# Expert layers: half of the first up product placed ahead of the last two picks, and the loop rotated behind it

## The chip, the cores and the metric

The kernel runs on one core of one Trainium2 chip. The metric is the device time of one execution in microseconds, given as the median of the timed runs; less is better. The engines are TensorE (PE, with its weight loads as PEld), VectorE (DVE), ScalarE (ACT), GpSimd (POOL) and SyncE (SP, which issues the loads).

## The reference

The program is two blocks of two layers each over 512 tokens of width 1024. The change touches only the mixture of experts that closes each layer of the second block. Cut to that part:

```python
def hier_moe(h, w_grp, b_grp, w_rt, b_rt, w_up, w_down):
    ...
    x_pad = jnp.zeros((rows, dm), h.dtype).at[dest].set(xt[tok])
    ...
    def expert_block(args):
        xb, e = args
        gate_up = xb @ w_up[e]
        a, u = jnp.split(gate_up, 2, axis=-1)
        return (jax.nn.silu(a) * u) @ w_down[e]
    ...
    y = y_pad.reshape(rows, dm)[dest] * w_sorted[:, None].astype(h.dtype)
    return jnp.zeros_like(xt).at[tok].add(y).reshape(bsz, length, dm)
```

Every token goes to 2 of 32 experts. An expert multiplies its tokens by an up matrix (1024 x 1024: 512 columns for the gate, 512 for the values), forms silu(gate) times value, and multiplies by a down matrix (512 x 1024). The first such layer works on 528 tokens (16 meta tokens and 512 others), the second on 512.

## The kernel before

`stage_experts` computes one such layer, and it stands twice in the program: layer 0 with five token tiles (`T` is 5), layer 1 with four. All 32 experts are computed one after the other for up to 64 tokens each (tokens beyond 64 go through a later part that runs only where there are some). Two experts are a pair, since 128 columns of a one-hot matrix pick the tokens of two experts at once.

The steps of a pair `p`, and who does them:

- VectorE compares slot numbers with a row of numbers (`match`, L3881) and adds the two maps (`join`, L3887, signal `onehot`): a one-hot matrix `row`.
- TensorE multiplies the tokens by `row` (`pick`, L3892): eight chunks of 128 channels, for each chunk `T` matmuls. Chunks 0 to 3 go to one PSUM bank (signal `turned[0]`), chunks 4 to 7 to another (`turned[1]`).
- VectorE copies a bank to SBUF with the norm's gain (`place(0)`, `place(1)`, L3897, signals `placed[0]`, `placed[1]`). The picked tokens then stand transposed in `xT`.
- For each of the two experts, TensorE does the up product in two halves of four chunks (`tensor_up`, L3903). Half 0 reads what `place(0)` wrote, half 1 what `place(1)` wrote. Behind half 0 the signal `half_up` rises, behind half 1 `up_ready`.
- ScalarE takes the Silu (L4127, signal `silu`), VectorE multiplies (L4210, signal `hid`), TensorE transposes (`tensor_hidden`, L3908), ScalarE copies (L4131, signal `h_placed`), TensorE does the down product (`tensor_down`, L3915, signal `dn_ready`), VectorE copies the result out of PSUM (L4223), and ScalarE issues two stores of it.

The order on each engine is written by hand. On TensorE the picks of the next pair are spread through the current one: two chunks behind an up product, two behind the transposes. Before the loop TensorE runs all eight picks of pair 0 in one go. The loop (`pe.Fori(0, 5)`, six experts in its body) then begins with half 0 of expert 0. `last_pair` is written out behind the loop.

On VectorE, ahead of its loop, stand `place(0)`, `place(1)`, the `join` for the next pair, and then `route.overflow` (18 small steps, L3803 to L3832), which works out which experts have more than 64 tokens. VectorE takes its instructions in order, so its loop, with the multiplication L4210 of expert 0, begins behind all of that.

SyncE issues the loads of the weights, also in order. Up weights have three buffers, each loaded in two halves of 2048 KB (L3460); down weights have two buffers, 2048 KB each (L3463). The loads of the first experts are issued during the routing. In the loop:

```python
def load_up(e, b):
    sp.wait_ge(half_up.sem, e + (half_up.base - 2))
    weights.load_up(sp, e, b, 0).then_inc(up_in[b][0].sem, 16)
    sp.wait_ge(up_ready.sem, e + (up_ready.base - 2))
    weights.load_up(sp, e, b, 1).then_inc(up_in[b][1].sem, 16)
```

So half 0 of expert 3 is loaded when expert 0 has done its half 0, half 1 when expert 0 has done its up product, and then the down weights of expert 2 when `dn_ready` of expert 0 has risen.

Of the kernel before, what the change touches and what calls it, by code (L numbers as in the profile page):

```python
# [37 lines left out]
NEXP, GROUPS, EPG, DFF = 32, 4, 8, 512  # L38
# [3804 lines left out]
def stage_experts(g, layer, tiles, keep, gw, dest, slot, over, weights, gains, route, finish):  # L3843
# [11 lines left out]
    up_in, dn_in, y_free = weights.up_in, weights.down_in, (y_free0, y_free1)  # L3855
    turned, placed = (turned0, turned1), (placed0, placed1)
# [42 lines left out]
    def tensor_up(n, b, half):  # L3899
        wv = up[b].rearrange("p k (s q c) -> p k q s c", s=2, q=2)  # L3900
        for k in range(4 * half, 4 * half + 4):
            for q in range(2):
                last = nc.tensor.matmul(g.psum[64 * q:64 * q + 64, 2 + n, :].rearrange("p (s c) -> p s c", s=2), xT[:, k // 4, k % 4, ROWS * n:ROWS * n + ROWS], wv[:, k, q, :, :], start=k == 0, stop=k == KD - 1)  # L3903
        return last
# [69 lines left out]
    with nc.Block() as block:  # L3974
# [39 lines left out]
        def _(pe):  # L4014
            route.tensor(pe)

            def expert(p, n, turn_up, turn_down, b, more):

                if n == 0:
                    pe.wait_ge(placed[0].sem, p + (placed[0].base + 1))  # L4020
                pe.wait_ge(up_in[b][0].sem, 16 * turn_up + (up_in[b][0].base + 16))
                tensor_up(n, b, 0).then_inc(half_up.sem, 1)
                if n == 0:
                    pe.wait_ge(placed[1].sem, p + (placed[1].base + 1))
                pe.wait_ge(up_in[b][1].sem, 16 * turn_up + (up_in[b][1].base + 16))
                tensor_up(n, b, 1).then_inc(up_ready.sem, 1)
                if more:
                    if n == 0:
                        pe.wait_ge(onehot.sem, p + (onehot.base + 2))
                    pick((4 * n, 4 * n + 1))  # L4030
                pe.wait_ge(hid.sem, 2 * p + (hid.base + n + 1))
                tensor_hidden().then_inc(h_turned.sem, 1)
                if more:
                    pick((4 * n + 2, 4 * n + 3)).then_inc(turned[n].sem, 1)
                pe.wait_ge(h_placed.sem, 2 * p + (h_placed.base + n + 1))
                pe.wait_ge(dn_in[n].sem, 16 * turn_down + (dn_in[n].base + 16))
                tensor_down(n, n).then_inc(dn_ready.sem, 1)

            def last_pair():

                p = PAIRS - 1
                first, second = NEXP - 2, NEXP - 1
                for half in range(2):
                    pe.wait_ge(placed[half].sem, p + (placed[half].base + 1))
                    pe.wait_ge(up_in[first % 3][half].sem, 16 * (first // 3) + (up_in[first % 3][half].base + 16))
                    last = tensor_up(0, first % 3, half)
                last.then_inc(up_ready.sem, 1)
                pe.wait_ge(up_in[second % 3][0].sem, 16 * (second // 3) + (up_in[second % 3][0].base + 16))
                tensor_up(1, second % 3, 0)
                pe.wait_ge(hid.sem, hid.base + first + 1)  # L4050
                tensor_hidden().then_inc(h_turned.sem, 1)
                pe.wait_ge(*gated.at(2))
                for n in range(2):
                    for i in range(4):
                        last = turn_gates(i, n, (n, i * P))
                if T > 4:
                    for n in range(2):
                        last = turn_gates(4, n, (5, n * P))
                last.then_inc(*g_turned.up())
                pe.wait_ge(up_in[second % 3][1].sem, 16 * (second // 3) + (up_in[second % 3][1].base + 16))  # L4060
                tensor_up(1, second % 3, 1).then_inc(up_ready.sem, 1)
                pe.wait_ge(h_placed.sem, h_placed.base + first + 1)
                pe.wait_ge(dn_in[0].sem, 16 * p + (dn_in[0].base + 16))
                tensor_down(0, 0).then_inc(dn_ready.sem, 1)
                pe.wait_ge(hid.sem, hid.base + second + 1)
                tensor_hidden().then_inc(h_turned.sem, 1)
                pe.wait_ge(h_placed.sem, h_placed.base + second + 1)
                pe.wait_ge(dn_in[1].sem, 16 * p + (dn_in[1].base + 16))
                tensor_down(1, 1).then_inc(dn_ready.sem, 1)
# [12 lines left out]
                    to_tokens(i, picked[1], y_last[1], False, True).then_inc(*combined.up())  # L4082

            pe.wait_ge(onehot.sem, onehot.base + 1)
            for n in range(2):
                pick(range(4 * n, 4 * n + 4)).then_inc(turned[n].sem, 1)
            with pe.Fori(0, 5) as i:
                for j in range(6):
                    expert(3 * i + j // 2, j % 2, 2 * i + j // 3, 3 * i + j // 2, j % 3, True)
            count = blocks_over(pe)  # L4090
            last_pair()

# [204 lines left out]
            sig.count = 16 * len(range(b, NEXP, 3))  # L4297
    for sig in dn_in:
        sig.count = 16 * PAIRS
    half_up.count = NEXP - 2  # L4300
    for sig in (up_ready, hid, silu, h_turned, h_placed, dn_ready, y_placed):
        sig.count = NEXP
    for sig in y_free:
# [872 lines left out]
```

## Time and profile before

| | |
|---|---|
| median of 3 runs | 2619.38 us |
| lowest and highest run | 2616.13 and 2620.86 us |
| span of the profiled execution | 2617.4 us (the profile gives no other time for this execution) |
| TensorE busy | 2477.6 us, 95% of the span |
| TensorE weight loads busy | 1381.7 us, 53% |
| VectorE, ScalarE, GpSimd busy | 1091.8, 627.1, 580.7 us |
| DMA | 531.89 MB, 203 GB/s in the mean |
| mean granted TensorE clock | 0.987 of full speed |

The busy times are sums over the whole program; the two expert layers lie near 1221 to 1724 us and 2126 to 2608 us of the span. A busy TensorE is not one at its peak, since matmuls are pipelined and their ends are modelled. In the timeline, rows of equal instructions are merged: the number behind the x is how many, and the length runs from the first one's start to the last one's end. One matmul of the program is two rows in the trace, as the picks show: 40 in the program's order, 80 in the timeline.

### The profile page before, as it was taken

The page shows a single profiled execution, that of the slowest core. Times are in us where ns is not written, and L with a number is a line of the kernel's source. Part 1 is how long each engine was busy: PE and PEld are TensorE (multiplying, and loading weights), DVE is VectorE, ACT ScalarE, POOL GpSimd, SP SyncE. Part 2 cuts the span into 40 slices and gives each one's busy share as a digit, 9 for nine tenths or more (in the row PEclk, how much of TensorE's full clock was granted, in tenths as well). Part 3 has the DMA queues.
Part 4 walks back from the last instruction along what each step waited for, and adds up shares of the span by engine and source line. Part 5 has one row for each costly group of instructions (what it writes and reads, how often), then busy time and mean ns, then how long its engine had stood idle before and what let it go on. Part 6 is the DMA issues. An engine that isn't in the chain of part 4 may idle for free. (4 is left out here: it accounts for less than half of the span.)

```text
span 2617.4 us, 38917 instructions
## 1 busy us (share of the span) xinstructions
PE 2477.6 (95%) x15572; PEld 1381.7 (53%) x15572; DVE 1091.8 (42%) x2083; ACT 627.1 (24%) x1451; POOL 580.7 (22%) x688
## 2 busy tenths in 40 slices
PE   7997899999989999999999999989999899999998
PEld 4554445756644444546555555558555454545443
DVE  4636554554255554755111211264666541111113
ACT  2217113433311222812000001032455121000010
POOL 1734343462124231430000000020345200000001
PEclk9999999999999999999999999999999999999999
DMA  5121013110120411154999999851001369999998
GB/s 190 65 96 49 33 37 129 53 36 3 35 81 10 155 65 66 50 213 177 403 426 427 428 426 426 359 196 65 34 34 66 131 247 425 426 426 428 426 427 364
DMA packets 116730, 531.89 MB, mean 203 GB/s; under 512 B 23601, under 2 KB 33713, under 8 KB 83825
## 3 DMA queue, kind: packets, MB, share of 16 engines
q1 hardware_dynamic: 104624, 505.74, 48.1%
q10 hardware_dynamic: 9600, 15.74, 1.6%
q0 software_dynamic: 2368, 8.52, 0.9%
q8 instruction: 94, 1.54, 0.2%
q14 instruction: 44, 0.35, 0.0%
HBM read 507.26 MB, written 22.58 MB: 202 GB/s over the span
## 5 line engine op out<-in xcount | busy, mean ns | idle before, releaser
L3903 PE MATMUL psum<-arena,hidden_T 128*64 128x512 f32 x1376 | 303.0, 592 | 0.0
L3892 PEld LDWEIGHTS psum<-hidden_T,arena 128*128 128x128 f32 x2304 | 266.6, 192 | 51.5 <-issue 51.5
L3892 PE MATMUL psum<-hidden_T,arena 128*128 128x128 f32 x2304 | 283.5, 278 | 1.2 <-DVE hidden_T L3887 1.2
L3915 PE MATMUL psum<-weight_ring,hidden_T 128*64 128x512 f32 x1024 | 233.7, 598 | 13.4 <-DMA weight_ring<-in_moe_w_down 10.1
L3903 PEld LDWEIGHTS psum<-arena,hidden_T 128*64 128x64 f32 x1376 | 100.6, 137 | 193.2 <-issue 193.1
L3897 DVE TENSOR_TENSOR hidden_T<-psum,norm_gains 128x512 f32<-128x512 f32 x64 | 44.3, 692 | 295.5 <-PE psum L3903 182.7
L4127 ACT ACTIVATE hidden_T<-psum 128x256 f32<-128x256 f32 x64 | 24.6, 385 | 530.5 <-PE psum L3903 530.5
L3903 PE MATMUL psum<-weight_ring,hidden_T 128*64 128x512 f32 x672 | 147.9, 592 | 0.0
L3915 PEld LDWEIGHTS psum<-weight_ring,hidden_T 128*64 128x64 f32 x1024 | 69.2, 136 | 131.6 <-issue 118.7
L4175 POOL DMA_INDIRECT arena<-expert_rows_out,arena x10 | 12.0, 1199 | 502.5 <-DMA expert_rows_out<-arena 499.7
L4573 PE MATMUL psum<-weight_ring,hidden_T 128*128 128x512 f32 x256 | 122.1, 606 | 0.3 <-DVE arena L4931 0.3
L4175 POOL DMA_INDIRECT weight_ring<-expert_rows_out,arena x8 | 8.1, 1012 | 483.6 <-DMA expert_rows_out<-arena 481.4
L337 POOL TENSOR_TENSOR arena<-arena,constants 128x1 f32<-128x1 f32 (+6 forms) x90 | 102.8, 1142 | 7.5
L4210 DVE TENSOR_TENSOR hidden_T<-hidden_T,psum 128x256 f32<-128x256 f32 x60 | 25.0, 416 | 186.5 <-ACT hidden_T L4127 186.5
L3903 PEld LDWEIGHTS psum<-weight_ring,hidden_T 128*64 128x64 f32 x672 | 49.0, 137 | 94.6 <-issue 94.5
L333 POOL TENSOR_SCALAR arena<-arena 128x1 f32<-128x1 f32 (+6 forms) x90 | 32.3, 359 | 286.7 <-DVE arena L3107 82.0
L4223 DVE COPY hidden_T<-psum 128x512 f32<-128x512 f32 x30 | 20.8, 692 | 179.8 <-PE psum L3915 179.8
L4127 ACT ACT_TABLE_LOAD x30 | 38.5, 1283 | 216.4 <-issue 216.3
L4769 POOL TENSOR_TENSOR weight_ring<-arena 128x256 f32<-128x256 f32 x56 | 41.7, 745 | 188.2 <-PE psum L4621 102.2
L445 PE MATMUL psum<-arena 128*128 128x512 f32 x160 | 70.6, 594 | 2.9 <-DVE hidden L550 2.9
L550 DVE TENSOR_TENSOR hidden<-hidden,psum 128x512 f32<-128x512 f32 x48 | 32.1, 684 | 95.1 <-PE psum L445 95.1
L347 PE MATMUL psum<-weight_ring,arena 128*128 128x512 f32 (+2 forms) x192 | 63.4, 454 | 6.0 <-PEq L1583 6.0
(646 smaller groups left out, 4391.6 us busy)
## 6 DMA issues: line engine op xcount, KB each, us to landing
arena<-in_moe_w_up SPq DMA_DIRECT2D x86, 2048.0 KB, 14.9
weight_ring<-in_moe_w_down SPq DMA_DIRECT2D x64, 2048.0 KB
weight_ring<-in_moe_w_up SPq DMA_DIRECT2D x42, 2048.0 KB, 14.8
weight_ring<-in_hg_w_in SPq DMA_DIRECT2D x8, 2048.0 KB, 11.6
weight_ring<-in_ev_w_in SPq DMA_DIRECT2D x8, 1536.0 KB, 8.9
weight_ring<-in_fox_w_in SPq DMA_DIRECT2D x6, 2048.0 KB, 11.8
weight_ring<-in_od_w_in SPq DMA_DIRECT2D x5, 2048.0 KB, 8.3
weight_ring<-in_ple_w_gate SPq DMA_DIRECT2D x4, 2048.0 KB, 8.9
```

The source lines that it names most:

```text
L333: g.nc.gpsimd.tensor_scalar(out, sums, scale, EPS, ALU.mult, ALU.add).then_inc(*chain.up())
L337: g.nc.gpsimd.tensor_tensor(out, out, power, ALU.pow).then_inc(*done.up())
L347: last = nc.tensor.matmul(out, l, r, start=i == 0, stop=i == len(left) - 1)
L445: last = nc.tensor.matmul(where[n](p), a[:, k, :], b[:, k, :], start=k == 0 and n in (1, 5, 6), stop=k == 3, skip_group_check=n in (2, 3, ...
L550: nc.vector.tensor_tensor(dst, dst, where[n](p), ALU.add).then_inc(*added.up())
L3892: last = nc.tensor.matmul(g.psum[:, c // 4, (c % 4) * P:(c % 4 + 1) * P], keep[:, i, c * P:(c + 1) * P], row[:, i, :], start=i == 0, stop= ...
L3897: return nc.vector.tensor_tensor(xT[:, a, :, :], g.psum[:, a, :].rearrange("p (k r) -> p k r", k=4), gain[:, 4 * a:4 * a + 4].unsqueeze(2) ...
L3903: last = nc.tensor.matmul(g.psum[64 * q:64 * q + 64, 2 + n, :].rearrange("p (s c) -> p s c", s=2), xT[:, k // 4, k % 4, ROWS * n:ROWS * n ...
L3915: last = nc.tensor.matmul(g.psum[64 * q:64 * q + 64, 6 + n, :], aT[:, k % 2, 64 * (k // 2):64 * (k // 2) + 64], down[b][:, k, 512 * q:512 ...
L4127: nc.scalar.activation(s, g.psum[:, 2 + n, 0:256], ACT.Silu).then_inc(silu.sem, 1)
L4573: last = mm(bank(u % 2), g.hT[:, k, a:a + n], w[:, k, :], **flags)
L4769: op(dv[:, :, 0, :], mid, bv[:, :, 0, :], ALU.subtract).then_inc(*subbed.up())
```

## The change

Ahead of the loop TensorE now runs picks 0 to 5, then half 0 of expert 0's up product, then picks 6 and 7. A function `first_half` holds half 0. In the loop body an expert that opens a pair begins with half 1, since its half 0 is done, and behind each expert that closes a pair half 0 of the next pair's first expert follows. `last_pair` begins with half 1 for the same reason, and half 0 of expert 30 now raises `half_up`, so its count is one higher. The parameter `more` was always true and is gone. No other engine's code is changed.

```diff
--- before.py
+++ after.py
@@ -4014,24 +4014,27 @@
         def _(pe):
             route.tensor(pe)
 
-            def expert(p, n, turn_up, turn_down, b, more):
+            def first_half(p, n, turn_up, b):
 
                 if n == 0:
                     pe.wait_ge(placed[0].sem, p + (placed[0].base + 1))
                 pe.wait_ge(up_in[b][0].sem, 16 * turn_up + (up_in[b][0].base + 16))
-                tensor_up(n, b, 0).then_inc(half_up.sem, 1)
+                return tensor_up(n, b, 0)
+
+            def expert(p, n, turn_up, turn_down, b):
+
                 if n == 0:
                     pe.wait_ge(placed[1].sem, p + (placed[1].base + 1))
+                else:
+                    first_half(p, n, turn_up, b).then_inc(half_up.sem, 1)
                 pe.wait_ge(up_in[b][1].sem, 16 * turn_up + (up_in[b][1].base + 16))
                 tensor_up(n, b, 1).then_inc(up_ready.sem, 1)
-                if more:
-                    if n == 0:
-                        pe.wait_ge(onehot.sem, p + (onehot.base + 2))
-                    pick((4 * n, 4 * n + 1))
+                if n == 0:
+                    pe.wait_ge(onehot.sem, p + (onehot.base + 2))
+                pick((4 * n, 4 * n + 1))
                 pe.wait_ge(hid.sem, 2 * p + (hid.base + n + 1))
                 tensor_hidden().then_inc(h_turned.sem, 1)
-                if more:
-                    pick((4 * n + 2, 4 * n + 3)).then_inc(turned[n].sem, 1)
+                pick((4 * n + 2, 4 * n + 3)).then_inc(turned[n].sem, 1)
                 pe.wait_ge(h_placed.sem, 2 * p + (h_placed.base + n + 1))
                 pe.wait_ge(dn_in[n].sem, 16 * turn_down + (dn_in[n].base + 16))
                 tensor_down(n, n).then_inc(dn_ready.sem, 1)
@@ -4040,11 +4043,9 @@
 
                 p = PAIRS - 1
                 first, second = NEXP - 2, NEXP - 1
-                for half in range(2):
-                    pe.wait_ge(placed[half].sem, p + (placed[half].base + 1))
-                    pe.wait_ge(up_in[first % 3][half].sem, 16 * (first // 3) + (up_in[first % 3][half].base + 16))
-                    last = tensor_up(0, first % 3, half)
-                last.then_inc(up_ready.sem, 1)
+                pe.wait_ge(placed[1].sem, p + (placed[1].base + 1))
+                pe.wait_ge(up_in[first % 3][1].sem, 16 * (first // 3) + (up_in[first % 3][1].base + 16))
+                tensor_up(0, first % 3, 1).then_inc(up_ready.sem, 1)
                 pe.wait_ge(up_in[second % 3][0].sem, 16 * (second // 3) + (up_in[second % 3][0].base + 16))
                 tensor_up(1, second % 3, 0)
                 pe.wait_ge(hid.sem, hid.base + first + 1)
@@ -4082,11 +4083,15 @@
                     to_tokens(i, picked[1], y_last[1], False, True).then_inc(*combined.up())
 
             pe.wait_ge(onehot.sem, onehot.base + 1)
-            for n in range(2):
-                pick(range(4 * n, 4 * n + 4)).then_inc(turned[n].sem, 1)
+            pick(range(4)).then_inc(turned[0].sem, 1)
+            pick((4, 5))
+            first_half(0, 0, 0, 0).then_inc(half_up.sem, 1)
+            pick((6, 7)).then_inc(turned[1].sem, 1)
             with pe.Fori(0, 5) as i:
                 for j in range(6):
-                    expert(3 * i + j // 2, j % 2, 2 * i + j // 3, 3 * i + j // 2, j % 3, True)
+                    expert(3 * i + j // 2, j % 2, 2 * i + j // 3, 3 * i + j // 2, j % 3)
+                    if j % 2:
+                        first_half(3 * i + j // 2 + 1, 0, 2 * i + (j + 1) // 3, (j + 1) % 3).then_inc(half_up.sem, 1)
             count = blocks_over(pe)
             last_pair()
 
@@ -4297,7 +4302,7 @@
             sig.count = 16 * len(range(b, NEXP, 3))
     for sig in dn_in:
         sig.count = 16 * PAIRS
-    half_up.count = NEXP - 2
+    half_up.count = NEXP - 1
     for sig in (up_ready, hid, silu, h_turned, h_placed, dn_ready, y_placed):
         sig.count = NEXP
     for sig in y_free:
```

On TensorE at the entry of layer 0's loop (names in brackets are the signals waited for: `rows_placed_0` and `rows_placed_1` are `placed`, `piece_loaded_0` and `piece_loaded_1` the two halves of the first up weights, `gated` is `hid`), before:

```order
L3892 MATMUL psum<-hidden_T,arena 128x128 [waits onehot_ready,rows_scaled]
L3892 MATMUL psum<-hidden_T,arena 128x128 x39
L4087 UNCONDITIONAL_BRANCH
L4087 ISA
L4021 ISA [waits rows_placed_0]
L3903 MATMUL psum<-weight_ring,hidden_T 64x512 [waits piece_loaded_0]
L3903 MATMUL psum<-weight_ring,hidden_T 64x512 x7
L3903 MATMUL psum<-weight_ring,hidden_T 64x512 [waits piece_loaded_1,rows_placed_1]
L3903 MATMUL psum<-weight_ring,hidden_T 64x512 x7
L4029 REGISTER_ALU
```

And now:

```order
L3892 MATMUL psum<-hidden_T,arena 128x128 [waits onehot_ready,rows_scaled]
L3892 MATMUL psum<-hidden_T,arena 128x128 x29
L3903 MATMUL psum<-weight_ring,hidden_T 64x512 [waits piece_loaded_0,rows_placed_0]
L3903 MATMUL psum<-weight_ring,hidden_T 64x512 x7
L3892 MATMUL psum<-hidden_T,arena 128x128 x10
L4090 UNCONDITIONAL_BRANCH
L4090 ISA
L4030 ISA [waits rows_placed_1]
L3903 MATMUL psum<-weight_ring,hidden_T 64x512 [waits piece_loaded_1]
L3903 MATMUL psum<-weight_ring,hidden_T 64x512 x7
```

Ten of the forty pick matmuls have moved behind the eight matmuls of half 0, and the wait for `rows_placed_1` has moved from a matmul in the middle of the up product to the sequencer, right behind the last picks and the branch into the loop.

On TensorE at the end of the same loop and the first rows of `last_pair` (L3959 reads the number of experts with more than 64 tokens), before:

```order
L3915 MATMUL psum<-weight_ring,hidden_T 64x512 [waits piece_loaded_7,hidden_placed]
L3915 MATMUL psum<-weight_ring,hidden_T 64x512 x7
L4087 REGISTER_ALU
L4087 COMPARE_AND_BRANCH
L3959 TENSOR_LOAD arena
L3959 ISA x2
L3903 MATMUL psum<-weight_ring,hidden_T 64x512 [waits piece_loaded_0,rows_placed_0]
L3903 MATMUL psum<-weight_ring,hidden_T 64x512 x7
```

And now:

```order
L3903 MATMUL psum<-weight_ring,hidden_T 64x512 [waits piece_loaded_0]
L3903 MATMUL psum<-weight_ring,hidden_T 64x512 x7
L4090 REGISTER_ALU
L4090 COMPARE_AND_BRANCH
L3959 TENSOR_LOAD arena
L3959 ISA x2
L3903 MATMUL psum<-weight_ring,hidden_T 64x512 [waits piece_loaded_1,rows_placed_1]
L3903 MATMUL psum<-weight_ring,hidden_T 64x512 x7
```

Half 0 of expert 30 (eight matmuls) has moved from behind the loop's closing branch and the read L3959 to ahead of them.

## Rows read from the trace of the kernel before

**Rows 1.** Timeline, ScalarE, both layers: start us, length us, engine, line, form, idle before.

```profile
1268.06 0.38 ACT L4127 ACTIVATE hidden_T<-psum 128x256 f32<-128x256 f32 x1 [3.24 <-PE psum L3903]
...
1298.72 0.39 ACT L4127 ACTIVATE hidden_T<-psum 128x256 f32<-128x256 f32 x1 [3.26 <-PE psum L3903]
...
2523.85 0.39 ACT L4127 ACTIVATE hidden_T<-psum 128x256 f32<-128x256 f32 x1 [3.25 <-PE psum L3903]
...
2554.57 0.38 ACT L4127 ACTIVATE hidden_T<-psum 128x256 f32<-128x256 f32 x1 [3.25 <-PE psum L3903]
```

**Rows 2.** Waits, TensorE, 1219 to 1700: who waited for whom: us, times, longest.

```profile
PE psum L3892 <- DVE hidden_T L3887: 0.9, 1, 0.9
```

**Rows 3.** Waits, TensorE, 2140 to 2617, columns as before.

```profile
PE psum L3915 <- DMA weight_ring<-in_moe_w_down: 10.1, 12, 1.0
```

**Rows 4.** Timeline, TensorE, the first wait for down weights in layer 1.

```profile
2405.65 3.65 PE L3915 MATMUL psum<-weight_ring,hidden_T 128*64 128x512 f32 x16 [0.57 <-DMA weight_ring<-in_moe_w_down]
```

**Rows 5.** Windows: stretch, length, busy us of PE, PEld, DVE, ACT, POOL; PEclk, DMA, GB/s.

```profile
2400.00:2545.00 145.00, 136.63 (x784) 72.20 (x782) 26.73 (x49) 12.83 (x24) 0.00 (x0) 1.00 1.01 427
```

**Rows 6.** Timeline, TensorE, entry of layer 0's expert loop.

```profile
1221.16 9.17 PE L3892 MATMUL psum<-hidden_T,arena 128*128 128x128 f32 x80 [0.91 <-DVE hidden_T L3887]
1230.26 7.09 PE L3903 MATMUL psum<-weight_ring,hidden_T 128*64 128x512 f32 x32
1237.28 2.50 PE L3892 MATMUL psum<-hidden_T,arena 128*128 128x128 f32 x20
1239.61 0.38 PE L3908 MATMUL psum<-constants,hidden_T 128*128 128x128 f32 x2
```

**Rows 7.** Timeline, TensorE, entry of layer 1's expert loop.

```profile
2126.82 7.38 PE L3892 MATMUL psum<-hidden_T,arena 128*128 128x128 f32 x64 [0.30 <-DVE hidden_T L3887]
2134.13 7.09 PE L3903 MATMUL psum<-arena,hidden_T 128*64 128x512 f32 x32
2141.15 2.05 PE L3892 MATMUL psum<-hidden_T,arena 128*128 128x128 f32 x16
2143.04 0.38 PE L3908 MATMUL psum<-constants,hidden_T 128*128 128x128 f32 x2
...
2148.62 7.04 PE L3903 MATMUL psum<-arena,hidden_T 128*64 128x512 f32 x32
```

**Rows 8.** Timeline, VectorE, entry of layer 0's expert loop.

```profile
1225.90 0.69 DVE L3897 TENSOR_TENSOR hidden_T<-psum,norm_gains 128x512 f32<-128x512 f32 x1 [2.37 <-PE psum L3892]
...
1230.37 0.69 DVE L3897 TENSOR_TENSOR hidden_T<-psum,norm_gains 128x512 f32<-128x512 f32 x1 [3.77 <-PE psum L3892]
...
1236.80 0.17 DVE L3832 CAST arena<-arena 128x17 int32<-128x17 f32 x1
1237.81 0.42 DVE L4210 TENSOR_TENSOR hidden_T<-hidden_T,psum 128x256 f32<-128x256 f32 x1 [0.84 <-ACT hidden_T L4127]
```

**Rows 9.** Timeline, VectorE, entry of layer 1's expert loop.

```profile
2134.24 0.69 DVE L3897 TENSOR_TENSOR hidden_T<-psum,norm_gains 128x512 f32<-128x512 f32 x1 [2.88 <-PE psum L3892]
...
2140.40 0.18 DVE L3832 CAST arena<-arena 128x17 int32<-128x17 f32 x1
2141.68 0.42 DVE L4210 TENSOR_TENSOR hidden_T<-hidden_T,psum 128x256 f32<-128x256 f32 x1 [1.11 <-ACT hidden_T L4127]
```

**Rows 10.** Timeline, SyncE's queue, the first down load of layer 1's loop.

```profile
2148.99 0.39 SPq L3463 DMA_DIRECT2D weight_ring<-in_moe_w_down  x1
```

**Rows 11.** Windows, right behind the first down load of layer 1's loop.

```profile
2150.00:2154.00 4.00, 4.00 (x22) 1.35 (x20) 0.00 (x0) 0.00 (x0) 0.00 (x0) 1.00 0.97 300
```

**Rows 12.** Timeline, TensorE, entry of the stage behind layer 0.

```profile
1737.37 1.97 PE L4621 MATMUL psum<-hidden_T,weight_ring 128*128 128x256 f32 x8 [1.64 <-PEq L3974]
```

**Rows 13.** Windows, within layer 1's routing.

```profile
2114.00:2118.00 4.00, 4.00 (x7) 1.61 (x6) 3.45 (x18) 1.07 (x2) 0.00 (x0) 0.57 0.99 420
```

**Rows 14.** Timeline, TensorE, 16 matmuls that hold the engine busy, layer 0 and layer 1.

```profile
1208.62 7.11 PE L359 MATMUL psum<-constants 128*128 128x512 f32 x16
...
2113.56 8.81 PE L359 MATMUL psum<-constants 128*128 128x512 f32 x16
```

## Prediction

> **What bounds the kernel now.** I looked first for the part of the span that the edit can touch: the two expert layers, some 480 us each. The Silu activations give the pace of an expert, since each expert has one. In layer 0 two experts take 1298.72 - 1268.06 = 30.66 us, and late in layer 1 they take 2554.57 - 2523.85 = 30.72 us [rows 1]. The paces are alike but the causes differ. In layer 0 TensorE waits once, 0.9 us, ahead of the first pick, and never again [rows 2], so the layer is as long as its matmuls. Layer 1 has four token tiles, not five, so its picks are shorter and its first expert needs only 2148.62 - 2134.13 = 14.49 us [rows 7]. It runs at its matmuls' pace until the first wait for down weights at 2405.65 [rows 4], and from there it has 12 such waits, 10.1 us in all [rows 3], at 427 GB/s [rows 5]. An expert moves three loads of 2048 KB and two stores of 128 KB, 6.55 MB, and 6.55 MB at 427 GB/s take 15.35 us, which is half of 30.70. So layer 0 is bound by TensorE, and layer 1 by a stream of loads that starts when its first buffers are given back.
>
> The place of the edit is the entry of each loop. There TensorE runs eight picks, then expert 0's up product in two halves, two picks, the hidden transposes (L3908), two picks, the down product. VectorE puts the picked blocks into place (`place(0)` and `place(1)`, L3897), then works through the overflow code (L3803 to L3832), and only then enters its own loop, whose first instruction is the gating product L4210 that the transposes wait for.
>
> **The change, part by part.** No matmul, load or copy is added or removed. What moves is the order at the entry, on TensorE alone; inside the loop the same order is written from another starting point.
>
> *Moved: first half ahead of the last two picks, layer 0.* The eight picks run from 1221.16 to 1230.26, 9.10 us, so two take 2.28 us. The up product runs from 1230.26 to 1237.28, so a half takes 3.51 us [rows 6]. In the new order the first half starts 2.28 us earlier, at 1227.98. Its operand is in place by then: `place(0)` ends at 1225.90 + 0.69 = 1226.59 [rows 8]. So this start costs no wait, and `half_up` rises 2.28 us earlier.
>
> *What it uncovers: `place(1)`.* Before, `place(1)` (0.69 us, from 1230.37, right behind the last pick) ran beside the first half, 3.51 us, and cost nothing [rows 6, 8]. Now the last picks stand behind the first half and end where the half ended before, near 1233.8, and the second half needs `place(1)` at once. Nothing is left on TensorE to cover it. I count 0.69 us for it; 0.11 us in front, since before it began that much behind the point at which TensorE could have gone on (1230.37 against 1230.26); and 0.1 us, an estimate from the same 0.11, for the hand-over back to TensorE: **0.9 us** of idle TensorE.
>
> *What is queued behind it on VectorE.* VectorE works in order, so the overflow code starts 3.51 us later too. Before, it ended at 1236.80 + 0.17 = 1236.97, 0.84 us ahead of L4210 [rows 8]; VectorE was waiting for the Silu. Now it ends at 1240.48. L4210 takes 0.42, so its product is there at 1240.90, and with 0.1 for the hand-over the transposes start at 1241.0, where they started at 1239.61 [rows 6]. That is a delay of **1.4 us**. The 0.9 us lie inside it: TensorE, 0.9 late, would have been at the transposes at 1240.5, and waits 0.5 more. The same sum for layer 1: the half is (2141.15 - 2134.13) / 2 = 3.51 us; the overflow code ends at 2140.40 + 0.18 + 3.51 = 2144.09; with 0.42 and 0.1 the transposes start at 2144.61 against 2143.04, **1.6 us** late [rows 7, 9].
>
> *The entry of VectorE's loop.* Branch and register work there was hidden in the idle time ahead of L4210, so the trace bounds it only: from nothing to 0.84 us (layer 0) and 1.10 us (layer 1, 2140.58 to 2141.68) [rows 8, 9]. I take 0.2 us in each layer, near the low end, for it is a few sequencer instructions. It adds 0.4 us in all.
>
> *Where the delay goes in layer 0.* TensorE sets the pace and has no idle time later to lose it in, so the whole 1.4 + 0.2 stays: +1.6 us.
>
> *Where it goes in layer 1, and what the early load is worth.* The load of expert 3's first half goes out when `half_up` rises, half an up product behind 2134.13, and would go out some 1.8 us earlier, two picks of layer 1 (2134.13 - 2126.82 = 7.31 us, a quarter of it) [rows 7]. The transfer can start then, since the queues are idle. But the queue that it stands in is in order: half 0 (behind `half_up`), half 1 (behind `up_ready`), then the down weights (behind `dn_ready` of expert 0). The last of these was issued at 2148.99 [rows 10], and the stretch right behind it shows 300 GB/s where a full stretch shows 427 [rows 5, 11]: the stream had run dry when the down load came, and stands full from then on. So the stream starts from `dn_ready`, which comes 1.6 + 0.2 us later. The 1.8 us gained at its head end as a gap in front of the down load. The stream is what layer 1 waits for at its end, so +1.8 us remain. The Trainium skill (DMA: Bandwidth & Descriptors, Rules for kernel authors) says to issue a DMA early and to wait for it late, so that its fixed cost overlaps. By that rule layer 1 would be 1.8 us faster, and it is the first rival; the low rate ahead of the down load speaks against it here.
>
> *The loop's other edge.* The branch back and the read of the overflow count now stand behind a half product of 3.51 us, before behind a down product of about as much (3.65 us with its drain) [rows 4]. The cover is alike, and the cost nothing; without it, it would show as a wait of PE's sequencer.
>
> **Sum.** 1.6 + 1.8 = 3.4 us later. The profiled execution spans 2617.4 us; the three runs have a median of 2619.38, 2.0 above it, and I add to the median: 2619.4 + 3.4 = **2622.8 us**. A measurement of this kernel tells a change from none at about 0.2%, 5.2 us, so this is 'same' with a lean to slower.
>
> **The rivals.**
> *The head start counts.* If the down load still found the stream full, and VectorE kept up, layer 1 would end 1.8 us earlier and layer 0 where it did: 2617.6 us. For it: the layer is bound by its loads, and the first of them goes earlier. Against: the dry stretch [rows 11], and `place(1)` with no cover. Chance 0.10.
> *The clock falls.* Slower than before by more than a measurement's error: two pauses of TensorE, 0.9 and 0.5 to 0.7 us, lie within some 7 us of each other. Behind a sparse stretch of layer 1's routing the granted clock averaged 0.57, so it was at 1.2 GHz for most of 2114 to 2118 [rows 13], and the same 16 matmuls took 8.81 us there and 7.11 in layer 0 [rows 14], 1.7 us more. One such fall in each layer gives 3.4 + 3.4 = 6.8 us: 2626.2. It decides if these pauses count as that stretch did. Against: 12 waits, 0.8 us in the mean, left the clock at 1.00 [rows 3, 5]. Chance 0.08.
> *TensorE pays for entering its loop.* The branch into the loop used to stand behind eight picks and now behind two, and the wait for `place(1)` holds the sequencer, not a matmul. Another block's entry showed 1.64 us of sequencer wait [rows 12]. Were all of it behind the 0.9 us, TensorE would be 2.5 us late in each layer, more than VectorE's 1.4 and 1.6: 5.0 us, 2624.4. Against: the first half and the two picks, 5.8 us, are queued when the branch is reached. The Trainium skill (Runtime: NRT & Kernel Launch, Instruction fetch mechanics) says that a taken branch to code that isn't at hand forces a fetch before execution goes on. By that rule this rival's time would come out; the loop's branch back shows no such pause in before. Chance 0.12.
> *Nothing arrives.* If the overflow code were faster or the hand-overs hidden, only part of 0.9 us per layer would show: 2619.4 to 2621.2, chance 0.15.
>
> **How the numbers follow.** The forecast has the remaining 0.55. Its own bounds are 0.9 us per layer (the copy alone) and 1.4 + 0.84 and 1.6 + 1.1 us (the loop entry at its bound), so 2621.2 to 2624.3. The range reaches to the rivals on both sides, and to it belongs the spread of the runs, 2616.1 to 2620.9: 2617.6 to 2626.5. Faster by over 0.2% would need more than both ways give: 0.03. Slower by over 0.2% has the clock's 0.08, and some of the loop entries' chance with the runs' spread: 0.18. The rest, 0.79, is within.
>
> **What would show it.** Right: in each layer the first half's row ahead of the last picks; TensorE idle for about 0.9 us behind VectorE's L3897 ahead of the second half, and again for 0.5 to 0.9 us ahead of the first L3908; L4210 straight behind L3832 and no longer behind the Silu; the down load issued 1.6 to 1.8 us later against the start of the picks; layer 0's pace still 30.66 us. Wrong: no idle time at the entry (the cover is longer than I think), a down load that isn't later, layer 1's stream without a gap ahead of it, a granted clock under 1.00 at the entry, or a wait of PE's sequencer there.

## The result and the profile after

The changed kernel takes 2623.59 us (median of 8 runs, 2619.93 to 2624.72), the kernel before 2617.09 us (8 runs beside it, 2613.28 to 2620.86). The ratio is 1.0023, 95% interval 1.0014 to 1.0031: about 6.0 us slower, 3.7 to 8.1. The forecast was 2622.8 us, its range 2617.6 to 2626.5. The ratio lies just above the bound of 0.2% that the chances were given for, and its interval holds that bound, so it isn't told on which side the change lies. That 2622.8 comes so near to 2623.59 is partly luck: the forecast stood on a median of 2619.38 us, 2.3 above the one measured here, and its change of 3.4 us lies just under the measured interval. The profiled execution took 2621.11 us, 1.9 above its span, at a mean granted clock of 0.985. Its page gives a span of 2619.2 us with TensorE busy for 2482.5 us, 4.9 more than before.

TensorE's timeline at the entry of layer 0's loop, which answers to [rows 6] (start us, length us, line, operands, count, and in brackets the idle time before and what ended it):

```profile
1222.15 6.93 PE L3892 MATMUL psum<-hidden_T,arena 128*128 128x128 f32 x60 [0.91 <-DVE hidden_T L3887]
1229.01 3.65 PE L3903 MATMUL psum<-weight_ring,hidden_T 128*64 128x512 f32 x16
1232.60 2.50 PE L3892 MATMUL psum<-hidden_T,arena 128*128 128x128 f32 x20
1235.97 3.65 PE L3903 MATMUL psum<-weight_ring,hidden_T 128*64 128x512 f32 x16 [0.87 <-DVE hidden_T L3897]
1239.55 2.50 PE L3892 MATMUL psum<-hidden_T,arena 128*128 128x128 f32 x20
1242.45 0.44 PE L3908 MATMUL psum<-constants,hidden_T 128*128 128x128 f32 x2 [0.40 <-DVE hidden_T L4215]
...
1248.53 7.04 PE L3903 MATMUL psum<-arena,hidden_T 128*64 128x512 f32 x32
```

And of layer 1's, for [rows 7]:

```profile
2128.79 5.60 PE L3892 MATMUL psum<-hidden_T,arena 128*128 128x128 f32 x48 [0.30 <-DVE hidden_T L3887]
2134.32 3.65 PE L3903 MATMUL psum<-arena,hidden_T 128*64 128x512 f32 x16
2137.90 2.05 PE L3892 MATMUL psum<-hidden_T,arena 128*128 128x128 f32 x16
2140.83 3.65 PE L3903 MATMUL psum<-arena,hidden_T 128*64 128x512 f32 x16 [0.88 <-DVE hidden_T L3897]
2144.41 2.05 PE L3892 MATMUL psum<-hidden_T,arena 128*128 128x128 f32 x16
2147.03 0.44 PE L3908 MATMUL psum<-constants,hidden_T 128*128 128x128 f32 x2 [0.57 <-DVE hidden_T L4215]
...
2152.67 7.04 PE L3903 MATMUL psum<-arena,hidden_T 128*64 128x512 f32 x32
```

The first half (x16) stands ahead of the last picks, and in each layer two waits stand where before there was none: 0.9 us for `place(1)`, and 0.4 or 0.57 us for the gating product ahead of the first transposes (L4215; it was L4210 before, since the change moves the lines behind it by five). From the first pick to the second expert's up product the entry takes 1248.53 - 1222.15 = 26.38 us in layer 0, and 23.88 in layer 1. Before, layer 1 had 2148.62 - 2126.82 = 21.80 [rows 7], and layer 0 had 1245.64 - 1221.16 = 24.48 [rows 6], with this row of the kernel before:

```profile
1245.64 7.04 PE L3903 MATMUL psum<-arena,hidden_T 128*64 128x512 f32 x32
```

So the entries are 1.90 and 2.08 us longer.

VectorE's timeline at the two entries, for [rows 8, 9]:

```profile
1235.13 0.69 DVE L3897 TENSOR_TENSOR hidden_T<-psum,norm_gains 128x512 f32<-128x512 f32 x1 [7.55 <-PE psum L3892]
1241.56 0.18 DVE L3832 CAST arena<-arena 128x17 int32<-128x17 f32 x1
1241.97 0.42 DVE L4215 TENSOR_TENSOR hidden_T<-hidden_T,psum 128x256 f32<-128x256 f32 x1 [0.23 <-DVE arena L3832]
...
2139.99 0.69 DVE L3897 TENSOR_TENSOR hidden_T<-psum,norm_gains 128x512 f32<-128x512 f32 x1 [6.66 <-PE psum L3892]
2146.14 0.17 DVE L3832 CAST arena<-arena 128x17 int32<-128x17 f32 x1
2146.55 0.42 DVE L4215 TENSOR_TENSOR hidden_T<-hidden_T,psum 128x256 f32<-128x256 f32 x1 [0.23 <-DVE arena L3832]
```

L4215 now follows L3832 by 0.23 us, and the bracket names VectorE itself; before it named the Silu, after 0.84 us of idle time [rows 8]. The engine that waited now makes others wait.

SyncE's queue at layer 1's entry (start us, length, line, transfer; x2 are the issues of half 0 and half 1), for [rows 10], the first row from before, the others from the change:

```profile
2138.39 3.37 SPq L3460 DMA_DIRECT2D arena<-in_moe_w_up  x2
...
2138.57 6.45 SPq L3460 DMA_DIRECT2D arena<-in_moe_w_up  x2
2153.04 0.39 SPq L3463 DMA_DIRECT2D weight_ring<-in_moe_w_down  x1
```

Behind the first pick, half 0 is issued at 9.78 us and the down load at 24.25. Before, half 0 went out at 2138.39, 11.57 us behind the first pick, and the down load at 2148.99, 22.17 behind. So half 0 goes 1.79 us earlier and the down load 2.08 later. Half 1, whose issue ends the x2 row, goes later too: 16.23 us behind the first pick, before 14.94. TensorE's waits in layer 1's loop, for [rows 3] (us in all, times, longest):

```profile
PE psum L3915 <- DMA weight_ring<-in_moe_w_down: 9.5, 11, 1.0
PE psum L3903 <- DVE hidden_T L3897: 0.9, 1, 0.9
PE psum L3908 <- DVE hidden_T L4215: 0.6, 1, 0.6
```

It still ends on the down weights, 9.5 us where it was 10.1 [rows 3]. The windows over the two entries and the late loop (stretch, length, busy us of PE, PEld, DVE, ACT, POOL, granted clock, DMA share, GB/s), for [rows 5]:

```profile
2400.00:2545.00 145.00, 138.17 (x785) 71.68 (x782) 25.45 (x47) 13.96 (x25) 0.00 (x0) 1.00 1.01 426
1222.00:1260.00 38.00, 36.58 (x242) 23.90 (x243) 12.96 (x36) 1.53 (x4) 0.00 (x0) 1.00 0.58 215
2128.00:2160.00 32.00, 30.25 (x183) 17.09 (x182) 12.00 (x36) 1.02 (x3) 0.00 (x0) 1.00 0.54 200
```

The clock was granted in full at both entries, and no bracket there names PE's sequencer.

### The profile page after: what moved, and what is told of

Same layout as the page of the kernel before. It is cut to its first block and busy times, and to the rows that moved or that the text cites. A ratio compares the mean times of both kernels' runs of the same rounds, so it can differ in the third digit from the quotient of the medians.

```text
span 2619.2 us, 38917 instructions
## 1 busy us (share of the span) xinstructions
PE 2482.5 (95%) x15572; PEld 1384.0 (53%) x15572; DVE 1090.3 (42%) x2083; ACT 626.1 (24%) x1451; POOL 580.6 (22%) x688
## 5 line engine op out<-in xcount | busy, mean ns | idle before, releaser
L3903 PE MATMUL psum<-arena,hidden_T 128*64 128x512 f32 x1376 | 303.2, 592 | 0.9 <-DVE hidden_T L3897 0.9
L3892 PEld LDWEIGHTS psum<-hidden_T,arena 128*128 128x128 f32 x2304 | 266.8, 192 | 53.1 <-issue 53.1
L3892 PE MATMUL psum<-hidden_T,arena 128*128 128x128 f32 x2304 | 284.0, 278 | 1.2 <-DVE hidden_T L3887 1.2
L3915 PE MATMUL psum<-weight_ring,hidden_T 128*64 128x512 f32 x1024 | 233.7, 598 | 10.5 <-DMA weight_ring<-in_moe_w_down 9.5
L3903 PEld LDWEIGHTS psum<-arena,hidden_T 128*64 128x64 f32 x1376 | 100.5, 137 | 193.6 <-issue 193.5
L3903 PE MATMUL psum<-weight_ring,hidden_T 128*64 128x512 f32 x672 | 148.1, 592 | 0.9 <-DVE hidden_T L3897 0.9
L3915 PEld LDWEIGHTS psum<-weight_ring,hidden_T 128*64 128x64 f32 x1024 | 69.2, 136 | 128.6 <-issue 116.5
L4215 DVE TENSOR_TENSOR hidden_T<-hidden_T,psum 128x256 f32<-128x256 f32 x60 | 24.9, 416 | 185.0 <-ACT hidden_T L4132 184.5
L3903 PEld LDWEIGHTS psum<-weight_ring,hidden_T 128*64 128x64 f32 x672 | 49.0, 137 | 95.1 <-issue 94.9
```

Source lines behind the costliest of these rows:

```text
L3892: last = nc.tensor.matmul(g.psum[:, c // 4, (c % 4) * P:(c % 4 + 1) * P], keep[:, i, c * P:(c + 1) * P], row[:, i, :], start=i == 0, stop= ...
L3915: last = nc.tensor.matmul(g.psum[64 * q:64 * q + 64, 6 + n, :], aT[:, k % 2, 64 * (k // 2):64 * (k // 2) + 64], down[b][:, k, 512 * q:512 ...
```

## The experiments

The theory: the half product was the cover of `place(1)`, and of the overflow code behind it on VectorE. Without that cover both layers' entries end later. Layer 0 keeps the delay, since TensorE bounds it; layer 1 keeps most of it, since its stream of loads starts from `dn_ready`. The rivals: the rotated loop itself costs something; the early load is worth something; the rest is the spread of the runs. No run moves the down load alone, so that layer 1's stream starts from `dn_ready` rests on the order of the queue and on the bytes below.

Seven kernels were run on two chips, each beside runs of the kernel before: four on one chip (before 2616.06 us, 35 runs), three on another (2616.89 us, 29 runs). From each profile I took the length of the two entries as above, and of the whole layers: from the first pick to L3935, behind the last down product (layer 0), and to the last long run of up products (layer 1). The table holds what each has more than the kernel before. The references are 24.48 and 21.80 us for the entries, 492.45 us for layer 0 and 451.35 us for layer 1. They stand in the profile of `e7_before_again`; the first profile of before has the same values to 0.02 us, but for layer 0's last pair, told of at the end. The rows at the ends, of layer 0 in `e7_before_again` (its start and its end) and in the change, then of layer 1 in before and in the change:

```profile
1224.24 9.17 PE L3892 MATMUL psum<-hidden_T,arena 128*128 128x128 f32 x80 [0.84 <-DVE hidden_T L3887]
1716.69 8.85 PE L3935 MATMUL psum<-arena 64*128 64x512 f32 x40
...
1716.50 8.85 PE L3935 MATMUL psum<-arena 64*128 64x512 f32 x40
...
2578.18 10.50 PE L3903 MATMUL psum<-arena,hidden_T 128*64 128x512 f32 x48
...
2581.63 10.50 PE L3903 MATMUL psum<-arena,hidden_T 128*64 128x512 f32 x48
```

| run | entry, layer 0 | entry, layer 1 | whole layer 0 | whole layer 1 | ratio, 95% interval |
|---|---|---|---|---|---|
| the change | +1.90 | +2.08 | +1.90 | +1.49 | 1.0023, 1.0014 to 1.0031 |
| e6: the change again | +1.90 | +2.07 | +1.90 | +1.58 | 1.0019, 1.0010 to 1.0028 |
| e1: rotation alone | 0.00 | 0.00 | 0.00 | +0.70 | 1.0003, 0.9994 to 1.0011 |
| e2: overflow code early | +1.36 | +1.36 | +1.35 | +1.01 | 1.0012, 1.0002 to 1.0021 |
| e3: `place(1)` in two parts | +0.35 | +0.35 | +0.35 | 0.00 | 1.0000, 0.9990 to 1.0009 |
| e4: both copies uncovered | +2.75 | +2.92 | +2.75 | +2.42 | 1.0021, 1.0012 to 1.0030 |
| e5: half 0 loaded late | 0.00 | 0.00 | 0.00 | +1.79 | 1.0003, 0.9994 to 1.0012 |
| e7: before again | 0 | 0 | 0 | 0 | 0.9994, 0.9983 to 1.0005 |

**e1_rotation_only.** The change's loop, but all eight picks ahead of the first half, as before.

```diff
-            pick(range(4)).then_inc(turned[0].sem, 1)
-            pick((4, 5))
+            for n in range(2):
+                pick(range(4 * n, 4 * n + 4)).then_inc(turned[n].sem, 1)
             first_half(0, 0, 0, 0).then_inc(half_up.sem, 1)
-            pick((6, 7)).then_inc(turned[1].sem, 1)
```

> All eight picks run ahead of half 0 again, as before the change; the loop still begins behind half 0. Theory (the cost is the lost cover of place(1) and the late overflow code, the rotation is free): the time from the first pick to the second expert's first up row is that of before, 24.5 us in layer 0 and 21.8 in layer 1, no wait of TensorE for L3897, and the ratio to before is 1.000 (0.999 to 1.001). Rival (the loop's new shape costs what the entry does not explain, some 2 us of the 6 measured): the entry rows as before, but the total 2 us longer, ratio 1.0008 or more.

Measured: 2615.93 us, ratio 1.0003. Both entries are as long as before to the hundredth. The whole layer 1 shows 0.70 us more in this one profile, though its loads ran level with those of before. TensorE waits there 13 times for down weights, 10.7 us in all, where it waited 12 times, 10.1 us [rows 3]; why, stays open. So a length of layer 1 out of one profile can be 0.7 us off. Writing the loop from another starting point costs nothing that shows; the cost is in the order of the prologue.

**e2_overflow_early.** The change, with the overflow code put between the two copies on VectorE, where it was idle for 7.55 us.

```diff
                 place(n).then_inc(placed[n].sem, 1)
+                if n == 0:
+                    route.overflow(dve)
             join().then_inc(onehot.sem, 1)
-            route.overflow(dve)
```

> The change, with VectorE's overflow code moved between place(0) and place(1), where VectorE sat idle 7.5 us. Theory: the waits of 0.40 and 0.57 us ahead of the first hidden transposes vanish, the wait of 0.87 us for place(1) stays; first pick to second expert 26.0 us in layer 0 and 23.3 in layer 1 (with the change 26.4 and 23.9, before 24.5 and 21.8); total about 1 us under the change, 3 over before, ratio 1.0011. Rival (VectorE's delay had no part): entry as with the change.

Measured: 2619.67 us, ratio 1.0012. TensorE's timeline at layer 0's entry:

```profile
1236.06 3.65 PE L3903 MATMUL psum<-weight_ring,hidden_T 128*64 128x512 f32 x16 [0.94 <-DVE hidden_T L3897]
...
1241.98 0.38 PE L3908 MATMUL psum<-constants,hidden_T 128*128 128x128 f32 x2
```

The wait ahead of the transposes is gone and the one for `place(1)` stands. The two terms are separate: the VectorE queue is worth 1.90 - 1.36 = 0.54 us in layer 0 and 0.72 in layer 1. Of the 1.36 that are left the wait is 0.94; about 0.4 us belongs to neither wait.

**e3_split_place.** e2, and `place(1)` in two copies of two chunks each. The last two picks go to a PSUM bank of their own, so that the copy of chunks 4 and 5 runs beside the first half. The edit is shown for TensorE's entry only; the loop, `last_pair` and VectorE's entry are split to match.

```diff
-            pick((4, 5))
+            pick((4, 5)).then_inc(*part_turned.up())
             first_half(0, 0, 0, 0).then_inc(half_up.sem, 1)
-            pick((6, 7)).then_inc(turned[1].sem, 1)
+            pick((6, 7), 7).then_inc(turned[1].sem, 1)
+            pe.wait_ge(*part_placed.at(1))
+            pe.wait_ge(up_in[0][1].sem, up_in[0][1].base + 16)
+            tensor_up_of(0, 0, (4, 5))
```

> As the run before, and place(1) of the first pair in two parts, the first right behind picks 4 and 5, the second behind picks 6 and 7, which go to another PSUM bank; a quarter of the up product (chunks 4 and 5) stands ahead of the loop and covers the second part. So half_up is as early as with the change, and no wait is uncovered. Theory (the early load is worth nothing): entry 24.5 to 25.1 us in layer 0 and 21.8 to 22.4 in layer 1 (before 24.5 and 21.8; some switches between picks and products more), total 0 to 1.2 us over before, ratio 1.000 to 1.0005. Rival (the early load gives layer 1 its 1.8 us): layer 1 from its first pick to the last expert's up product 1.8 us shorter than the 451.4 us of before, ratio 0.9993.

Measured: 2615.88 us, ratio 1.0000. TensorE at layer 0's entry (L3893, L3910 and L3915 are L3892, L3903 and L3908 of the change):

```profile
1223.50 6.94 PE L3893 MATMUL psum<-hidden_T,arena 128*128 128x128 f32 x60 [0.91 <-DVE hidden_T L3888]
1230.37 3.65 PE L3910 MATMUL psum<-weight_ring,hidden_T 128*64 128x512 f32 x16
1233.95 2.50 PE L3893 MATMUL psum<-hidden_T,arena 128*128 128x128 f32 x20
1236.38 3.65 PE L3910 MATMUL psum<-weight_ring,hidden_T 128*64 128x512 f32 x16
1239.96 2.50 PE L3893 MATMUL psum<-hidden_T,arena 128*128 128x128 f32 x20
1242.30 0.38 PE L3915 MATMUL psum<-constants,hidden_T 128*128 128x128 f32 x2
```

No wait is left, the half still starts 2.2 us earlier (1.8 in layer 1), and half 0's load in layer 1 is issued 9.78 us behind the first pick as in the change. Yet the entry is 0.35 us longer than before. The matmuls are the same; the order alternates once more between picks and products. The two last picks take 1236.38 - 1233.95 = 2.43 us to the next row, where the forecast counted 2.28; all eight take 6.87 + 2.43 = 9.30, before 9.10, and the two halves 7.16, before 7.02. This is about the part that belonged to no wait in e2. That the alternation makes it, and not the split's other parts, is the likely reading; no run separates them. And with the whole head start kept and no wait to pay for it, layer 1 is as long as before: against its own entry, 0.35 us longer, the head start gave back 0.35 of 1.79. The ratio alone couldn't say so, since its interval also holds the rival's 0.9993.

**e4_both_uncovered.** The change, with the first half ahead of picks 4 to 7, so that `place(0)` loses its cover as well.

```diff
             pick(range(4)).then_inc(turned[0].sem, 1)
-            pick((4, 5))
             first_half(0, 0, 0, 0).then_inc(half_up.sem, 1)
-            pick((6, 7)).then_inc(turned[1].sem, 1)
+            pick(range(4, 8)).then_inc(turned[1].sem, 1)
```

> Half 0 one step further ahead: picks 0 to 3, half 0, then picks 4 to 7. Theory: now place(0) has no cover either, a second wait of 0.87 us in each layer on top of the change's; first pick to second expert 27.2 us in layer 0 and 24.7 in layer 1; total 1.7 us over the change's, 5.5 to 7.5 over before, ratio 1.002 to 1.003. half_up rises 3.6 us earlier than before in layer 0. Rival (an earlier load pays): layer 1 loses less than layer 0 by the lead gained, and the total is under that of the change.

Measured: 2621.00 us, ratio 1.0021. TensorE at layer 0's entry shows one more wait of the same kind:

```profile
1227.24 3.65 PE L3903 MATMUL psum<-weight_ring,hidden_T 128*64 128x512 f32 x16 [0.78 <-DVE hidden_T L3897]
1230.83 4.73 PE L3892 MATMUL psum<-hidden_T,arena 128*128 128x128 f32 x40
1236.43 3.65 PE L3903 MATMUL psum<-weight_ring,hidden_T 128*64 128x512 f32 x16 [0.87 <-DVE hidden_T L3897]
...
1242.91 0.44 PE L3908 MATMUL psum<-constants,hidden_T 128*128 128x128 f32 x2 [0.40 <-DVE hidden_T L4214]
```

The second uncovered copy adds 0.78 us of waiting and 0.85 us of entry over the change. Half 0's load goes out 8.84 us behind the first pick, 0.94 earlier than in the change, and layer 1 is 2.42 us longer than before all the same. The total was expected some 1.7 us over the change's; the ratios, 1.0021 against 1.0023 and 1.0019, don't show that difference.

**e5_late_half.** The kernel before, with the load of every half 0 held back until the whole up product is done. No engine's order of work changes.

```diff
-                sp.wait_ge(half_up.sem, e + (half_up.base - 2))
+                sp.wait_ge(up_ready.sem, e + (up_ready.base - 2))
                 weights.load_up(sp, e, b, 0).then_inc(up_in[b][0].sem, 16)
```

> The kernel before, with the load of each half 0 held back until the whole up product is done (both halves behind up_ready). TensorE's order is untouched, so only the loads move, 3.5 us later at the entry. Theory (in layer 1 the start of a stream without gaps counts; a load matters by the gap it leaves ahead of the first down load): first pick to second expert 24.5 and 21.8 us as before, layer 0 unchanged, layer 1 from its first pick to the last expert's up product some 1.5 us over the 451.4 to 452.1 of before, no stretch without traffic ahead of the first down load; total 1.5 us over before, ratio 1.0006. Rival (the first load's time is worth nothing in either direction): layer 1 as before, 451.4 to 452.1. Rival (it is worth its whole time): 3.5 us more.

Measured: 2617.84 us, ratio 1.0003. SyncE's queue at layer 1's entry:

```profile
2139.81 0.92 SPq L3460 DMA_DIRECT2D arena<-in_moe_w_up  x2
2147.75 0.39 SPq L3463 DMA_DIRECT2D weight_ring<-in_moe_w_down  x1
```

With its first pick at 2125.19, half 0 goes out at 14.62 us, 3.05 later than before, and the down load at 22.56. Layer 1 is 1.79 us longer, which the ratio can't tell from nothing. So 3.05 us of lateness cost 1.79; the stream had some 1.26 us of slack ahead of the down load, not more. An issue that comes later costs more here than one that comes earlier gives.

**e6_change_again** and **e7_before_again.** Both kernels unaltered, to have a second profile of each and a time of before against itself.

> The change itself, unaltered, a second time, to see what the entries leave over. Theory: its entries cost 1.9 us in layer 0 and, in layer 1, 2.1 us of which the early load gives 0.6 to 0.7 back, 3.3 to 3.4 us in all, ratio 1.0013; the 1.0023 measured first is the upper part of its interval. Rival (something else costs 2 to 3 us more): ratio 1.0023 again, and longer stretches outside the two entries.

> The kernel before, unaltered, against itself, to see what a ratio of this size is worth. Expected: ratio 1.000 with an interval of about 0.0009 either way; entries 24.5 and 21.8 us, layer 1 from first pick to the last up product 451.4 to 452.1 us; the last down product's wait for ScalarE 0.5 us, where the profile of before showed 1.3 and 2.1.

Measured: the change 2622.03 us, ratio 1.0019; before 2616.50, ratio 0.9994. The change's entries and layers repeat to 0.1 us. Before against itself comes out 0.06% low, with an interval of 0.11% on either side: differences of that size are not told apart here.

**Where layer 1's stream loses.** The bytes moved since the first pick, added up from windows of 1 us, tell when each kernel has moved as many as before. Minus is ahead of before, in us:

| us behind the first pick | change | e6 | e3 | e4 | e5 | e7 |
|---|---|---|---|---|---|---|
| 15 | -1.7 | -1.7 | -1.8 | -2.6 | +3.1 | 0.0 |
| 20 | -0.6 | -0.5 | -1.4 | +0.4 | +3.2 | 0.0 |
| 30 | +1.6 | +1.7 | 0.0 | +2.6 | +1.9 | -0.1 |
| 40 | +1.3 | +1.4 | -0.1 | +2.3 | +1.8 | -0.2 |
| 200 | +1.4 | +1.5 | -0.1 | +2.4 | +1.9 | -0.2 |
| 390 | +1.5 | +1.6 | 0.0 | +2.4 | +1.8 | -0.2 |

The change is ahead at first, by its head start, as the rival had it, and has lost it all by 30 us. It loses it in two steps: 1.1 us by 20 us, where half 1's load goes out 1.29 us later than before, and 2.2 us more ahead of the down load. From there the lag stays within 0.3 us for 360 us. The second step's gap, in windows of 1 us up to where the first down load's data come in, of before:

```profile
2148.82:2149.82 1.00, 1.00 (x6) 0.29 (x4) 0.69 (x1) 0.00 (x0) 0.00 (x0) 1.00 1.03 442
2149.82:2150.82 1.00, 1.00 (x8) 0.34 (x6) 0.00 (x0) 0.00 (x0) 0.00 (x0) 1.00 1.02 205
2150.82:2151.82 1.00, 1.00 (x8) 0.38 (x6) 0.00 (x0) 0.00 (x0) 0.00 (x0) 1.00 0.69 221
```

and of the change:

```profile
2150.79:2151.79 1.00, 1.00 (x6) 0.29 (x4) 0.00 (x0) 0.00 (x0) 0.00 (x0) 1.00 0.60 246
2151.79:2152.79 1.00, 1.00 (x8) 0.41 (x6) 0.00 (x0) 0.00 (x0) 0.00 (x0) 1.00 0.00 0
2152.79:2153.79 1.00, 1.00 (x8) 0.31 (x6) 0.69 (x1) 0.00 (x0) 0.00 (x0) 1.00 0.00 0
2153.79:2154.79 1.00, 1.00 (x6) 0.29 (x4) 0.00 (x0) 0.00 (x0) 0.00 (x0) 1.00 0.74 131
```

Before, the rate dips to 205 and 221 GB/s but never to nothing: (427 - 205) + (427 - 221) = 428, about one microsecond's worth of a full stream. In the change two whole windows move nothing, and the four together lack 181 + 427 + 427 + 296 = 1331, or 3.1 us.

## Why the prediction was right, and where it was off

**`place(1)` uncovered: right.** The forecast was 0.9 us of idle TensorE per layer; it is 0.87 and 0.88. e4 shows nearly the same price for the other copy, 0.78.

**The overflow code queued behind it: right, a size off.** The forecast had the transposes 0.5 us late behind the first wait in layer 0, with 0.2 more for the loop's entry. The wait is 0.40 there and 0.57 in layer 1, and e2 takes it away by moving that code alone. The entry of VectorE's loop, which the trace of before could only bound between 0 and 0.84, shows as 0.23 us; 0.2 was taken.

**The delay at the entries: mis-sized.** The term was 1.4 + 0.2 in layer 0 and 1.6 + 0.2 in layer 1; measured are 1.90 and 2.08. The part that failed is "the overflow code starts 3.51 us later". `place(1)` starts 1235.13 - 1222.15 = 12.98 us behind the first pick, where it was 1230.37 - 1221.16 = 9.21 [rows 6, 8]: 3.77 later, and 3.78 in layer 1. A row that is cut out of a long run of like matmuls costs more than its share: to the point where VectorE begins, 80 picks in one run took 9.21 us, but 60 and 20 apart take 6.86 + 2.53 = 9.39. With the half at 3.59 for 3.51 that makes the 0.26 that lack. e3 shows such a part by itself: 0.35 us per layer with no wait in either.

**Layer 0 keeps its delay: right.** Entry +1.90, whole layer +1.90. TensorE had no idle time to lose it in.

**Layer 1 and the early load: right in kind, mis-sized.** The words "the stream had run dry" were too strong. It dipped, by one microsecond's worth, and half 1's tail was still moving when the down load went out. The down load is 2.08 us late, and the layer 1.5, so by the difference some 0.6 us of the head start of 1.79 did count, where the forecast gave it nothing. The same difference is 0.35 in e2 and e3 and 0.5 in e4 and e6, and e1 shows that one profile can be 0.7 off: something counts, how much is not settled. The forecast also left out that half 1 goes later, which took the first 1.1 us of the lead. The two errors cancel, by luck: 1.9 + 1.5 = 3.4 us, which is the sum that the forecast had, by 1.6 + 1.8.

**The rivals.** *The head start counts* falls in its size: e3 keeps the head start without the waits, its layer 1 is as long as before and not 1.8 us shorter, and the table of bytes shows the lead lost by 30 us. The Trainium skill (DMA: Bandwidth & Descriptors, Rules for kernel authors) says to issue a DMA early and to wait late, so that the fixed cost overlaps; the 1.8 us that the forecast put beside that rule don't come out, since the next transfers in the queue wait for buffers that come back no earlier. *The clock falls* falls: 1.00 in the windows of both entries. *TensorE pays for entering its loop* falls: the change's wait there is 0.87 us and names VectorE, none names the sequencer, and e3, with two picks and a quarter of the product ahead of the branch, has no idle time there. The Trainium skill (Runtime: NRT & Kernel Launch, Instruction fetch mechanics) says that a taken branch to code out of reach forces a fetch before execution goes on; no pause of 1.64 us, the price that the forecast put beside that rule, shows here. *Nothing arrives* falls with the table.

**What stays open.** The layers account for 3.4 us, 0.13%. The two measurements of the change gave 0.23% and 0.19%, with lower ends at 0.14% and 0.10%. The stretch between the two layers took 407.7 to 412.4 us in the profiles, with the same code in all, 412.3 in both profiles of the change and 412.4 and 408.0 in the two of before. For e2 to e5 the layers' sums (2.4, 0.4, 5.2, 1.8 us: 0.09, 0.01, 0.20, 0.07%) lie inside their intervals.

Much of the spread goes with the granted clock: over the 64 runs of before beside the experiments, a run is about 1.3 us longer for each 0.001 by which its mean granted clock is lower. A straight line through all 146 runs of the experiments, one slope for all, sets the kernels beside each other at an equal clock. By this estimate, good to 0.9 us either way, e1 is 0.0 us over before, e2 2.5, e3 0.3, e4 5.3, e5 2.6, e6 4.7 and e7 -0.4. The layers' sums agree with it but for the change itself: 4.7 us against 3.5 in e6's layers. So e5's cost is told from nothing, and e3 from the rival's gain of 1.8 us. Some 1.2 us of the change, a little more than the error, are in no row looked at, and their cause stays open.

## What to carry to other kernels

Work that stands between a producer and its consumer may be cover for a copy on another engine; before it is moved, ask what runs beside it and what is queued behind that copy on its engine. An earlier load is worth only as much as the next transfer in its queue can follow: where that one waits for a buffer which the same change gives back later, the lead becomes a gap. A short run cut out of a long run of like matmuls can cost more than its share, here some 0.35 us for one more alternation.

## What was not expected

Layer 0's last pair is 0.8 us longer in the first profile of before than in every other profile, that of the same kernel in e7 included, and layer 1's is 1.6 us longer. TensorE's timeline of the first profile of before, at the last down product of each layer:

```profile
1710.85 3.65 PE L3915 MATMUL psum<-weight_ring,hidden_T 128*64 128x512 f32 x16 [1.29 <-ACT hidden_T L4131]
...
2599.37 3.65 PE L3915 MATMUL psum<-weight_ring,hidden_T 128*64 128x512 f32 x16 [2.06 <-issue]
```

and of the change, in layer 1:

```profile
2601.23 3.65 PE L3915 MATMUL psum<-weight_ring,hidden_T 128*64 128x512 f32 x16 [0.47 <-ACT hidden_T L4136]
```

ScalarE's copy L4131, which this product needs, began late in that one execution, at 1710.41 and 2598.93 (the second bracket doesn't name it). The waits are 0.82 and 1.59 us over 0.47; without these 2.4 us the two profiled spans would lie 4.2 us apart, not 1.8. A sum against one profiled execution inherits such delays, so a second profile of the same kernel is worth its run.

What a load's time of issue is worth was not the same in both directions: 0.35 to 0.6 us for 1.79 us earlier (e3, the change), and 1.79 us for 3.05 later (e5). The slack ahead of the down load was about a microsecond, too small to be called a dry stretch.
